# Dense products with plain fp32 operands instead of fp32r high and low parts

## The chip, the cores and the metric

The kernel runs on one core of a Trainium2 chip. The metric is the device time of one execution in microseconds. The kernel before takes 3159.32 us, the median of two runs (3153.93 and 3164.72).

## The reference

The input is 512 tokens of width 1024 in fp32. Two hybrid layers come first. Each does, with D = 1024:

```python
mod = (c @ w_ada + b_ada)                      # shifts, scales, gains from a condition vector
h = rms_norm(x) * (1 + sc_m) + sh_m
proj = h @ w_in                                # to lru, q_down, kv_down, k_rope, gate_a, gate_b
y_a = rg_lru(causal_depthwise_conv(x_lru, ...), ...)   # block gates 128x128, a scan over time
y_b = mla(q_down, kv_down, k_rope, ...)        # 8 heads, up-projections w_uq, w_ukv, softmax
x = x + g_m * ((sigmoid(gate_a) * y_a + sigmoid(gate_b) * y_b) @ w_out)
h = rms_norm(x) * (1 + sc_f) + sh_f
gate, up = split(h @ w_ffn_in)                 # 2 x 2816 columns
x = x + g_f * ((silu(gate) * up) @ w_ffn_out)
```

A second block follows: a mixer (an mLSTM of 4 heads and a pooling branch between dense products w_in_2 and w_out_2), and a mixture of 32 experts of which each token takes 4, with a SwiGLU of width 1024 in each.

## The kernel before

Activations lie transposed: 8 tiles of 128 features by 512 tokens. A dense product is made in groups: one PSUM bank takes 128 output features x 512 tokens and accumulates over 8 (down-projection: 11) blocks of 128 input features. A **chunk** of weights is 1 MB (128 x 2048 floats, two groups of 8 products), 128 x 1408 floats for the down-projection.

**High and low parts.** TensorE gets its dense operands as fp32r tiles, in two parts: the high part is a copy to fp32r, the low part is the difference. A product is three matmuls, `split3` (L187 to L191): high x high, high x low, low x high. For weights, ScalarE copies the chunk from `RAW` to `WHI` (`high`, L147) and VectorE subtracts into `WLO` (`low`, L157). `RAW` has 4 slots of 8 KB per partition, `WHI` and `WLO` 3 each. SP loads a chunk when VectorE's `low` of the chunk 4 places before is done. `feed(n + 2)` on both engines keeps the parts two chunks ahead of TensorE, and stands in each engine's program between the other work of chunk n.

For activations, ScalarE and VectorE do the same at each place: after the norms (`nh`, `HH`, `HL`, L340 to L348 and L564 to L574), for the compressed queries and keys (`cqh`, `cql`, `ckvh`, `ckvl`), for the heads' result (`yh`, `yl`), for the hidden tiles of the feed-forward (`hidh`, `hidl`, L492 and L765), and in the mixer (L1404, L1533, L1670 to L1673, L1689).

**Order.** Each engine has one program in written order, and semaphores carry the dependencies. TensorE in a layer (`layer_pe`): four lru chunks with the block gates between them (`gates`, L839; its matmul at L848 has plain fp32 operands), q, kv, four ga, four gb chunks, the value up-projection (8 products of `ckv` by token), then 8 heads, each with five `split3` products for the queries and keys of the head two later, scores, transposes and values with plain fp32 operands; four `out` chunks, column sums for the norm (`stat`, L196), 11 `fi` chunks, 8 `fo` chunks, and both again for the second half of the hidden width. The wait for `ffl` (L958) of the last hidden tile stands before each `fo` group; the wait for `yl` of the last head (L943) before `out`.

Between the weight chunks lie chunks of `w_ada`, whose columns VectorE makes (`ada`, L513) and TensorE adds up (L822). The block weights `lruw` are loaded at chunk 4 of a layer, after the previous layer's last product. POOL writes zeros into the result buffer and prepares the experts' bias terms. The mixer (`mix_program`) goes in the same way through 15 chunks: gate, 4 qk, 2 v (256 columns a product), 2 u, 2 o, 4 out.

The expert loop (`moe_pe`, products at L2274) has 50 blocks of 64 tokens. Each block has 8 chunks for gate and up and 4 for down, with 4 matmuls of plain fp32 operands in each chunk.

Of the kernel before, what the change touches and what calls it, by code (L numbers as in the profile page):

```python
# [17 lines left out]
F32R = mybir.dt.float32r  # L18
# [8 lines left out]
P = 128  # L27
D = 1024
S = 512
# [28 lines left out]
RAW_SLOTS, W_SLOTS = 4, 3  # L58
# [58 lines left out]
class Part:  # L117

    def __init__(self, sg, l, chunks, prev, used, hi):
        self.sg, self.l, self.chunks, self.prev, self.used, self.hi = sg, l, chunks, prev, used, hi  # L120
        self.pieces = [c for c in chunks if c[2]]
        self.position = {c[:2]: n for n, c in enumerate(chunks)}
        self.ada = [c[:2] for c in chunks if not c[2]]
        self.ada_after = {chunks[n - 1][:2]: self.ada.index(c[:2]) for n, c in enumerate(chunks) if not c[2]}
        self.raw_from = prev.raw_from + len(prev.chunks) if prev else 0
        self.w_from = prev.w_from + len(prev.pieces) if prev else 0
# [4 lines left out]
    def w(self, n):  # L131
        return (n + self.w_from) % W_SLOTS

    def raw_free(self, n):

        if n >= RAW_SLOTS:
            return [self.sg.event(self.used, n - RAW_SLOTS)]
        return [self.prev.sg.event(self.prev.used, len(self.prev.chunks) + n - RAW_SLOTS)] if self.prev else []

    def w_free(self, n):  # L140

        if n >= W_SLOTS:
# [12 lines left out]


def low(v, m, L, n):  # L157

    kind, i, _ = L.pieces[n]
    c, size = L.position[kind, i], FLOATS.get(kind, SLOT)  # L160
    v.wait_ge(*L.sg.event(L.hi, n))
    v.tensor_tensor(m["WLO"][:, L.w(n), 0:size], m["RAW"][:, L.raw(c), 0:size],  # L162
                    m["WHI"].bitcast(F32)[:, L.w(n), 0:size], ALU.subtract).then_inc(*L.sg.inc(L.used, c, also=[("w", n)]))


AHEAD = 2
# [40 lines left out]
def log1p(v, sg, sem, out, u, s, p):  # L207
# [20 lines left out]
LAYER_SIGNALS = """step_act step_dve raw_in0 raw_in1 raw_in2 raw_in3 vec_in lruw_in raw_used w_hi pe_step  # L228
    act_free dve_free act_out dve_out act_sq act_root act_hi dve_h dve_lo act_exp act_pt act_qk
    dve_max dve_p dve_qa dve_pt dve_y ada_out"""  # L230


def layer_loads(sp, L, start, m, W):
# [11 lines left out]
    for n, (kind, i, _) in enumerate(L.chunks):  # L245
# [61 lines left out]
FLOATS = {"fo": NF * P}  # L307
# [3 lines left out]
def layer_act(act, L, after, start, m, b):  # L311
    K, X, HH, sg = m["K"], m["X"], m["HH"], L.sg

    fed = [AHEAD if L.prev else 0]

    def feed(upto):

        while fed[0] <= min(upto, len(W_CHUNKS) - 1):
            high(act, m, L, fed[0])
            fed[0] += 1  # L320
# [7 lines left out]
    def norm(t, eps):  # L328
# [11 lines left out]
        for k in range(KD):  # L340
            if t == 0 and not L.prev and k in (0, 4):
                feed(k // 4)
            act.wait_ge(*sg.event("dve_h", ("n", t, k)))
            if k >= 2:
                act.wait_ge(*sg.event("hl", (t, k - 2)))
# [37 lines left out]
    for n, (kind, i, _) in enumerate(W_CHUNKS):  # L383
        if kind == "uq":
            break
        feed(n + 2)
# [24 lines left out]
        elif kind == "ga":  # L411
# [5 lines left out]
            if i == 1:  # L417
# [4 lines left out]
                act.wait_ge(*sg.event("cq"))  # L422
                act.activation(m["cqh"][:], m["qraw"][:], ACT.Copy)
                act.activation(m["ckvh"][:], m["kvraw"][:], ACT.Copy).then_inc(*sg.inc("act_hi", "cq"))
# [7 lines left out]
    feed(W_INDEX["ukv", 0])  # L432
# [4 lines left out]

    def rounded(h):

        act.wait_ge(*sg.event("y", h))  # L440
        act.activation(m["yh"][:, h, :], m["ya"][:, h, :], ACT.Copy).then_inc(*sg.inc("act_hi", ("y", h)))


    for h in range(-2, HEADS):
# [19 lines left out]
        if h >= 0:  # L464
# [6 lines left out]
            if h:  # L471
                rounded(h - 1)
            if h >= 6:
                feed(W_INDEX["out", h - 6])
    rounded(HEADS - 1)
    act.activation(m["warm"][:], K[:, K_ONE:K_ONE + 1], ACT.Sqrt)
    for i in range(4):
        feed(W_INDEX["out", i] + 2)
# [4 lines left out]
    for q in range(2 * NF):  # L483
        half, j = divmod(q, NF)
        feed(W_INDEX["fi", q] + 2)
# [5 lines left out]
        act.wait_ge(*sg.event("ff_hid", q))  # L491
        act.activation(m["hidh"][:, j, :], m["fh"][:, q % 2, :], ACT.Copy).then_inc(*sg.inc("act_hi", ("ff", q)))  # L492
        if j == NF - 1:
            if half:
                act.activation(m["warm"][:], K[:, K_ONE:K_ONE + 1], ACT.Sqrt)
            for jj in range(KD):
                feed(W_INDEX["fo", half * KD + jj] + 2)
                if half and jj:
                    act.wait_ge(*sg.event("dve_free", FIRST_GROUP["fo", KD + jj - 1]))
                    square(2, jj - 1)  # L500
                if half and jj >= KD - AHEAD:
                    high(act, m, after, jj - KD + AHEAD)
    act.wait_ge(*sg.event("dve_free", FIRST_GROUP["fo", 2 * KD - 1]))
    square(2, KD - 1)


def layer_dve(v, L, after, start, m, b):
    f = lambda t: t.bitcast(F32)
    K, X, HH, HL, vec, mod, sg = m["K"], m["X"], m["HH"], m["HL"], m["vec"], m["mod"], L.sg

    fed, nw = [AHEAD if L.prev else 0], [AHEAD if L.prev else 0]

    def ada():  # L513

        c = fed[0]
        r = L.ada.index(L.chunks[c][:2])
# [12 lines left out]
        fed[0] += 1  # L529

    def feed(upto):


        while nw[0] <= min(upto, len(W_CHUNKS) - 1):
            if not L.chunks[fed[0]][2]:
                ada()
                continue
            low(v, m, L, nw[0])
            nw[0] += 1
            fed[0] += 1  # L540
# [12 lines left out]
    def norm(t):  # L553
# [10 lines left out]
        for k in range(KD + 1):  # L564
            if k < KD:
                if k >= 2:
                    v.wait_ge(*sg.event("act_hi", ("h", t, k - 2)))
                v.tensor_tensor(m["nt"][:, k % 2, :], X[:, k, :], root[:], ALU.mult).then_inc(*sg.inc("dve_h", ("n", t, k)))
            if t == 0 and not L.prev and k in (1, 5):
                feed(k // 4)  # L570
            if k:
                v.wait_ge(*sg.event("act_hi", ("h", t, k - 1)))
                v.tensor_tensor(HL[:, k - 1, :], m["nh"][:, (k - 1) % 2, :], f(HH)[:, k - 1, :],  # L573
                                ALU.subtract).then_inc(*sg.inc("dve_lo", ("h", t, k - 1), also=[("hl", (t, k - 1))]))  # L574
# [68 lines left out]
    for n, (kind, i, _) in enumerate(W_CHUNKS):  # L643
# [14 lines left out]
        elif kind == "ga":  # L658
# [4 lines left out]
            if i == 1:  # L663
# [3 lines left out]
                for j in range(2):  # L667
                    v.scalar_tensor_tensor(m["qraw"][:, j, :], m["qraw"][:, j, :], vec[:, V_QG + j:V_QG + j + 1],
                                           m["rq"][:, 0, :], ALU.mult, ALU.mult)
                v.scalar_tensor_tensor(m["kvraw"][:], m["kvraw"][:], vec[:, V_KVG:V_KVG + 1], m["rq"][:, 1, :],  # L670
                                               ALU.mult, ALU.mult).then_inc(*sg.inc("dve_out", "cq", also=[("cq", None)]))
                v.wait_ge(*sg.event("cq"))
                v.wait_ge(*sg.event("act_hi", "cq"))
                v.tensor_tensor(m["cql"][:], m["qraw"][:], f(m["cqh"])[:], ALU.subtract)
                v.tensor_tensor(m["ckvl"][:], m["kvraw"][:], f(m["ckvh"])[:], ALU.subtract).then_inc(*sg.inc("dve_lo", "cq", also=[("cql", None)]))
# [9 lines left out]

    def low_y(h):

        v.wait_ge(*sg.event("act_hi", ("y", h)))
        v.tensor_tensor(m["yl"][:, h, :], m["ya"][:, h, :], f(m["yh"])[:, h, :], ALU.subtract).then_inc(*sg.inc("dve_lo", ("y", h), also=[("yl", h)]))


    for h in range(-2, HEADS):
# [25 lines left out]
        if h >= 0:  # L718
# [6 lines left out]
            if h:  # L725
                low_y(h - 1)
# [6 lines left out]
    low_y(HEADS - 1)  # L733
# [17 lines left out]
    for q in range(2 * NF):  # L751
# [5 lines left out]
        if q >= 2:  # L757
            v.wait_ge(*sg.event("act_hi", ("ff", q - 2)))
# [1700 lines left out]
```

## Time and profile before

| | |
|---|---|
| median of the runs | 3159.32 us |
| profiled execution | 3160.7 us, span 3159.0 us |
| granted clock of TensorE, mean | 0.957 |
| TensorE matmul busy | 2889.7 us, 91% |
| TensorE weight load busy | 1776.6 us, 56% |
| VectorE busy | 1243.8 us, 39% |
| ScalarE busy | 748.3 us, 24% |
| GpSimd busy | 111.2 us, 4% |
| moved by DMA | 638.66 MB, mean 202 GB/s |

All times are of one profiled execution. A busy time is the union over an engine's records. Matmul records are from start to modelled end and overlap when matmuls follow each other, so the mean of a group is longer than the distance between two starts. Layer 0 reaches its first dense product at 63.02 us, the second layer follows at about 826 us, the mixer at about 1607 us, the expert loop at about 1895 us, and the last block ends at about 3115 us.

### The profile page before, as it was taken

To read this page: it belongs to the slowest core of one execution; us is meant where nothing else is said; L and a number is where in the kernel's file an instruction comes from. 1 tells how busy PE (TensorE), PEld (TensorE's weight loads), DVE (VectorE), ACT (ScalarE), POOL (GpSimd) and SP (SyncE) were. 2 spreads that over 40 slices of the span, in tenths; PEclk is the share of its full clock that TensorE was granted. 3 is DMA by queue.
4 is the path that set the end of the run, shared out by engine and by line. 5 is a ranking of instruction groups with operands and counts; after the bars stand their busy time and mean duration, and the time that the engine had idled before them with its cause. 6 is when DMAs were issued, how large, how long until landed. Compare 5 with 4: busy or idle time off the path is not lost.

```text
span 3159.0 us, 36442 instructions
## 1 busy us (share of the span) xinstructions
PE 2889.7 (91%) x13284; PEld 1776.6 (56%) x13284; DVE 1243.8 (39%) x2119; ACT 748.3 (24%) x1068; POOL 111.2 (4%) x171
## 2 busy tenths in 40 slices
PE   6997899999999899999998979999998999998984
PEld 5775578887778667788776763333332333332221
DVE  6883656765484454334266531111111111111113
ACT  3633432122373334222232320000000000000001
POOL 0020000000000000000010000000000000000001
PEclk7999999999999999999988979999999999999997
DMA  7264136664314022242322059594699979979995
GB/s 234 80 215 132 56 109 183 193 190 124 107 56 118 14 67 67 78 116 77 90 68 85 14 200 383 202 380 150 239 408 410 395 304 408 410 301 410 410 410 197
DMA packets 392991, 638.66 MB, mean 202 GB/s; under 512 B 28400, under 2 KB 278384, under 8 KB 392896
## 3 DMA queue, kind: packets, MB, share of 16 engines
q1 hardware_dynamic: 374784, 590.76, 52.3%
q0 software_dynamic: 9376, 31.14, 2.8%
q10 hardware_dynamic: 8736, 15.47, 1.4%
q8 instruction: 63, 1.03, 0.1%
q14 instruction: 32, 0.26, 0.0%
HBM read 610.77 MB, written 26.54 MB: 202 GB/s over the span
## 4 chain that ended last, share of the span: by engine, by line
PE 72%; DVE 7%; SPq 7%; DMA 7%; ACT 5%; issue 2%; POOL 0%; ACTq 0%; DVEq 0%; another core or an unknown queue 0%
PE bank L2274 24%; PE bank L189 13%; PE bank L191 12%; PE bank L190 12%; SPq L2164 5%; DMA ring<-w_down 4%; DMA ring<-w_gate 2%; PE bank L196 1%; PE bank L2279 1%; PE bank L899 1%; PE bank L900 1%; SPq L295 1%; PE bank L2266 1%; PE bank L940 1%; DVE WLO L162 1%
## 5 line engine op out<-in xcount | busy, mean ns | idle before, releaser
L2274 PE MATMUL bank<-ring,xT 128*64 128x512 f32 x3200 | 717.7, 595 | 43.8 <-DMA ring<-w_gate 21.6
L189 PE MATMUL bank<-HH,WHI 128*128 128x512 f32 x1360 | 551.5, 406 | 34.4 <-DVE HL L573 24.8
L190 PE MATMUL bank<-HL,WHI 128*128 128x512 f32 x1360 | 534.9, 393 | 0.0
L191 PE MATMUL bank<-HH,WLO 128*128 128x512 f32 x1360 | 534.5, 393 | 0.0
L2274 PEld LDWEIGHTS bank<-ring,xT 128*64 128x64 f32 x3200 | 220.1, 137 | 490.9 <-issue 384.6
L2274 PE MATMUL bank<-ring,hT 128*64 128x512 f32 x1600 | 360.0, 595 | 27.5 <-DMA ring<-w_down 25.8
L162 DVE TENSOR_TENSOR WLO<-RAW,WHI 128x2048 fp32r<-128x2048 f32 (+1 forms) x133 | 283.1, 2128 | 134.5 <-ACT WHI L154 134.4
L189 PEld LDWEIGHTS bank<-HH,WHI 128*128 128x128 f32 x1360 | 258.5, 190 | 108.4 <-DVE HL L573 20.4
L154 ACT ACTIVATE WHI<-RAW 128x2048 fp32r<-128x2048 f32 (+1 forms) x133 | 236.6, 1779 | 238.3 <-PE bank L191 177.5
L190 PEld LDWEIGHTS bank<-HL,WHI 128*128 128x128 f32 x1360 | 259.6, 191 | 54.0 <-issue 3.7
L191 PEld LDWEIGHTS bank<-HH,WLO 128*128 128x128 f32 x1360 | 258.8, 190 | 55.2
L2237 DVE TENSOR_SCALAR gc<-bank 128x512 f32<-128x512 f32 x50 | 34.6, 692 | 616.1 <-PE bank L2274 606.9
L2274 PEld LDWEIGHTS bank<-ring,hT 128*64 128x64 f32 x1600 | 108.5, 137 | 263.2 <-issue 195.6
L2217 ACT ACTIVATE ysb<-bank 128x512 f32<-128x512 f32 x50 | 29.9, 597 | 729.0 <-PE bank L2274 729.0
L2240 DVE TENSOR_SCALAR uc<-bank 128x512 f32<-128x512 f32 x50 | 34.6, 692 | 405.4 <-PE bank L2274 405.4
L189 PE MATMUL bank<-hidh,WHI 128*128 128x512 f32 x352 | 142.5, 405 | 11.8 <-DVE hidl L765 11.8
L524 DVE SCALAR_TENSOR_TENSOR acc<-RAW,c,acc 128x256 f32<-128x256 f32 x280 | 135.8, 485 | 10.0
L190 PE MATMUL bank<-hidl,WHI 128*128 128x512 f32 x352 | 139.6, 396 | 0.0
L191 PE MATMUL bank<-hidh,WLO 128*128 128x512 f32 x352 | 139.5, 396 | 0.0
L2210 ACT ACTIVATE th<-gc 128x512 f32<-128x512 f32 x50 | 31.6, 631 | 420.9 <-DVE gc L2237 420.9
L741 DVE SCALAR_TENSOR_TENSOR X<-bank,mod,X 128x512 f32<-128x512 f32 x48 | 36.0, 750 | 180.4 <-PE bank L191 180.4
L760 DVE SCALAR_TENSOR_TENSOR fh<-fth,bank 128x512 f32<-128x512 f32 x44 | 30.3, 688 | 165.1 <-PE bank L191 116.7
(397 smaller groups left out, 2920.5 us busy)
## 6 DMA issues: line engine op xcount, KB each, us to landing
ring<-w_gate SPq DMA_DIRECT2D x128, 1024.0 KB, 11.7
ring<-w_up SPq DMA_DIRECT2D x128, 1024.0 KB, 14.3
ring<-w_down SPq DMA_DIRECT2D x128, 1024.0 KB, 15.9
RAW<-w_ffn_in SPq DMA_DIRECT2D x88, 512.0 KB, 5.2
RAW<-w_ada SPq DMA_DIRECT2D x40, 1024.0 KB, 5.3
RAW<-w_in SPq DMA_DIRECT2D x37, 1024.0 KB, 5.6
RAW<-w_ffn_out SPq DMA_DIRECT2D x32, 704.0 KB, 4.7
expert_results<-ysb ACTq DMA_DIRECT2D x102, 128.0 KB, 5.5
```

Of the source, the lines that this page charges most:

```text
L154: act.activation(m["WHI"][:, L.w(n), 0:size], m["RAW"][:, L.raw(c), 0:size], ACT.Copy).then_inc(*L.sg.inc(L.hi, n))
L162: v.tensor_tensor(m["WLO"][:, L.w(n), 0:size], m["RAW"][:, L.raw(c), 0:size], m["WHI"].bitcast(F32)[:, L.w(n), 0:size], ALU.subtract).then ...
L189: pe.matmul(out, lhi, rhi, start=start, stop=False)
L190: pe.matmul(out, lhi, rlo, start=False, stop=False)
L191: return pe.matmul(out, llo, rhi, start=False, stop=stop)
L524: ins = v.scalar_tensor_tensor(acc, raw[:, k * 256:(k + 1) * 256], m["c"][:, k:k + 1], acc, ALU.mult, ALU.add)
L741: v.scalar_tensor_tensor(X[:, k, :], b[(g + j) % 4][:], mod[:, gain + k:gain + k + 1], X[:, k, :], ALU.mult, ALU.add).then_inc(*sg.inc("dv ...
L2164: return sp.dma_start(m["ring"][:, c, :].rearrange("p (k n) -> p k n", k=2), w[:, 2 * a:2 * a + 2, :])
L2210: act.activation(m["th"][:], m["gc"][:], ACT.Tanh, scale=SWIGLU_ALPHA / 2).then_inc(*sg.inc("mo_act", also=[("th", None)]))
L2237: v.tensor_scalar(gc, b[0][:], SWIGLU_LIMIT, None, ALU.min).then_inc(*sg.inc("mo_dve", also=[("gc", None)]))
L2240: v.tensor_scalar(uc, b[1][:], SWIGLU_LIMIT, -SWIGLU_LIMIT, ALU.min, ALU.max).then_inc(*sg.inc("mo_dve", also=[("uc", None)]))
L2274: ins = pe.matmul(out[halves(h), :], xT[:, k % 4, halves(k // 4)], m["ring"][:, c, at:at + 512], start=False, stop=k == KD - 1)
```

## The change

All dense products take plain fp32 operands, one matmul in the place of the three. `WHI`, `WLO` and all high and low parts of activations go, and so do `high`, `low`, `split3` and the copies and subtractions. `RAW` gets ten slots of 8 KB, in the place of 4 + 3 + 3. TensorE waits for a chunk's DMA itself and frees its slot; only ada chunks are freed by VectorE. The norm writes `H` with one ScalarE activation in the place of two. The first group of `out` waits for each head's `y`, the first group of `fo` for each hidden tile. `lruw` is loaded at chunk 8 in the place of 4, the mixer's small tables at chunk 9 in the place of 4, and its pool and router weights before ("o", 1) in the place of ("u", 1). The expert part stays.

```diff
-RAW_SLOTS, W_SLOTS = 4, 3
+RAW_SLOTS = 10
...
+    def chunk_used(self, n):
+
+        kind, i, dense = self.chunks[n]
+        return self.sg.event("w_used", self.index[kind, i]) if dense else self.sg.event("raw_used", n)
...
+    def weights(self, pe, m, n):
+
+        kind, i, _ = self.pieces[n]
+        c = self.position[kind, i]
+        pe.wait_ge(*self.sg.event("raw", c))
+        return m["RAW"][:, self.raw(c), :]
...
-def split3(pe, out, lhi, llo, rhi, rlo, start, stop):
-
-    pe.matmul(out, lhi, rhi, start=start, stop=False)
-    pe.matmul(out, lhi, rlo, start=False, stop=False)
-    return pe.matmul(out, llo, rhi, start=False, stop=stop)
...
-        if n == 4:
+        if n == LRUW_AT:
...
-            h = dict(scale=m["mod"][:, scale + k:scale + k + 1], bias=m["mod"][:, shift + k:shift + k + 1])
-            act.activation(m["nh"][:, k % 2, :], m["nt"][:, k % 2, :], ACT.Identity, **h)
-            act.activation(HH[:, k, :], m["nt"][:, k % 2, :], ACT.Identity, **h).then_inc(*sg.inc("act_hi", ("h", t, k)))
+            act.activation(H[:, k, :], m["nt"][:, k % 2, :], ACT.Identity, scale=m["mod"][:, scale + k:scale + k + 1],
+                           bias=m["mod"][:, shift + k:shift + k + 1]).then_inc(*sg.inc("act_h", ("h", t, k)))
...
-                if norm is not None and j == 0:
-                    pe.wait_ge(*sg.event("hl", (norm, k)))
-                ins = split3(pe, out[:], hi[:, c:c + P], lo[:, c:c + P], xh[:, k, :], xl[:, k, :], k == 0, k == KD - 1)
+                if first is not None and j == 0:
+                    pe.wait_ge(*first(k))
+                ins = pe.matmul(out[:], w[:, c:c + P], x[:, k, :], start=k == 0, stop=k == KD - 1)
...
-    pe.wait_ge(*sg.event("yl", KD - 1))
     for i in range(4):
-        dense("out", i, m["yh"], m["yl"])
+        dense("out", i, m["ya"], first=None if i else lambda k: sg.event("y", k))
...
-            pe.wait_ge(*sg.event("ffl", half * NF + NF - 1))
             for k in range(NF):
-                c = k * P
-                ins = split3(pe, out[:], hi[:, c:c + P], lo[:, c:c + P], m["hidh"][:, k, :], m["hidl"][:, k, :], k == 0, k == NF - 1)
+                if j == 0:
+                    pe.wait_ge(*sg.event("ff_hid", half * NF + k))
+                ins = pe.matmul(out[:], w[:, k * P:(k + 1) * P], m["hid"][:, k, :], start=k == 0, stop=k == NF - 1)
...
-            if n == RAW_SLOTS:
+            if n == RAW_SLOTS - 1:
                 sp.wait_ge(*L.prev.sg.event("dve_free", FIRST_GROUP["fo", 2 * KD - 1]))
...
-            if (kind, i) == ("u", 1):
+            if (kind, i) == ("o", 1):
                 sp.wait_ge(*sg.event("pre", 7))
...
-        pool.wait_ge(*sg.event("hl", KD - 1))
+        pool.wait_ge(*sg.event("h", KD - 1))
```

## Rows read from the trace of the kernel before

**Rows 1.** The page: busy time by engine, and lines of the chain that ended last

```profile
PE 2889.7 (91%) x13284; PEld 1776.6 (56%) x13284; DVE 1243.8 (39%) x2119; ACT 748.3 (24%) x1068; POOL 111.2 (4%) x171
...
PE bank L2274 24%; PE bank L189 13%; PE bank L191 12%; PE bank L190 12%; SPq L2164 5%; DMA ring<-w_down 4%; DMA ring<-w_gate 2%; PE bank L196 1%; PE bank L2279 1%; PE bank L899 1%; PE bank L900 1%; SPq L295 1%; PE bank L2266 1%; PE bank L940 1%; DVE WLO L162 1%
```

**Rows 2.** Windows: busy us (x instructions) by engine, granted clock, DMA share, GB/s

```profile
63.00:1860.00 1797.00, 1688.30 (x7532) 1345.83 (x7533) 984.04 (x1583) 630.14 (x862) 36.27 (x49) 0.96 0.35 102
...
1895.00:3115.00 1220.00, 1146.52 (x5500) 384.07 (x5499) 177.95 (x350) 86.19 (x152) 57.88 (x99) 1.00 0.87 341
```

**Rows 3.** Groups by shape: the first product of each triple

```profile
L189 PE MATMUL bank<-HH,WHI 128*128 128x512 f32 x1360 | 551.5, 406 | 34.4 <-DVE HL L573 24.8 <-DVE HL L1533 4.1 <-DVE HL L1673 2.7
...
L189 PE MATMUL bank<-hidh,WHI 128*128 128x512 f32 x352 | 142.5, 405 | 11.8 <-DVE hidl L765 11.8
...
L189 PE MATMUL bank<-yh,WHI 128*128 128x512 f32 x128 | 52.2, 408 | 9.6 <-DVE yl L689 9.6
...
L189 PE MATMUL bank<-cqh,WHI 128*128 128x512 f32 x64 | 26.4, 412 | 1.9 <-ACT V L436 1.9
...
L189 PE MATMUL bank<-WHI,ckvh 128*128 128x512 f32 x16 | 7.8, 490 | 19.0 <-DVE WLO L162 14.1 <-issue 4.9
...
L189 PE MATMUL bank<-WHI,HH 128*128 128x256 f32 x64 | 18.1, 283 | 0.0
```

**Rows 4.** Timeline (start us, duration us) of the output projection, layer 0

```profile
400.36 0.39 PE L189 MATMUL bank<-yh,WHI 128*128 128x512 f32 x1
...
409.20 0.39 PE L189 MATMUL bank<-yh,WHI 128*128 128x512 f32 x1
```

**Rows 5.** Plain fp32: line L848, its weight loads in time, and L2274

```profile
L848 PE MATMUL bank<-xc,lruw x64: 590/592/593, 92.8 to 918.9; 128*128 128x512 f32 x64
...
93.20 0.19 PEld L848 LDWEIGHTS bank<-xc,lruw 128*128 128x128 f32 x1 [0.24 <-issue]
...
95.77 0.19 PEld L189 LDWEIGHTS bank<-HH,WHI 128*128 128x128 f32 x1 [0.24 <-issue]
...
L2274 PE MATMUL bank<-ring,xT 128*64 128x512 f32 x3200 | 717.7, 595 | 43.8 <-DMA ring<-w_gate 21.6
```

**Rows 6.** The page's groups: VectorE's subtractions and ScalarE's copies of weights

```profile
L162 DVE TENSOR_TENSOR WLO<-RAW,WHI 128x2048 fp32r<-128x2048 f32 (+1 forms) x133 | 283.1, 2128 | 134.5 <-ACT WHI L154 134.4
...
L154 ACT ACTIVATE WHI<-RAW 128x2048 fp32r<-128x2048 f32 (+1 forms) x133 | 236.6, 1779 | 238.3 <-PE bank L191 177.5
```

**Rows 7.** TensorE's waits: line <- releaser: us in total, times, longest us

```profile
PE bank L189 <- DVE HL L573: 24.8, 16, 8.3
...
PE bank L189 <- DVE WLO L162: 15.6, 2, 14.1
...
PE bank L189 <- DVE hidl L765: 11.8, 4, 3.1
...
PE bank L1757 <- ACT row L1429: 10.9, 1, 10.9
...
PE bank L189 <- DVE yl L689: 9.6, 2, 6.2
...
PE bank L189 <- issue: 4.9, 1, 4.9
...
PE bank L189 <- DVE HL L1533: 4.1, 5, 2.4
```

**Rows 8.** The longest wait of SP's DMA queue

```profile
SPq L295 <- DVE WLO L162: 922.2, 104, 107.5
```

**Rows 9.** Windows with low clock, same columns as Rows 2

```profile
250.00:275.00 25.00, 9.95 (x37) 7.82 (x36) 7.30 (x6) 12.46 (x15) 0.72 (x1) 0.73 0.92 271
...
385.00:437.00 52.00, 51.40 (x245) 43.39 (x245) 22.70 (x30) 12.36 (x12) 0.00 (x0) 0.95 0.49 142
...
1700.00:1800.00 100.00, 89.13 (x390) 66.09 (x391) 53.20 (x153) 35.39 (x66) 0.00 (x0) 0.90 0.10 32
```

**Rows 10.** DMA issues: count, KB each, median us to landing

```profile
RAW<-w_in SPq DMA_DIRECT2D x37, 1024.0 KB, 5.6
```

More of the change, by code:

```diff
@@ L306, with layer_act @@
 Q_ORDER = (1, 0, 2, 3)
-FLOATS = {"fo": NF * P}
 SCALE = (NOPE + ROPE) ** -0.5
[L311 to L320, printed above, removed]
+def layer_act(act, L, start, m, b):
+    K, X, H, sg = m["K"], m["X"], m["H"], L.sg
     def square(t, k):
@@ L490, in layer_act, with layer_dve @@
         act.activation(m["fth"][:, q % 2, :], b[g % 4][:], ACT.Tanh, scale=0.5).then_inc(*sg.inc("act_out", ("ff_tanh", q)))
[L491 to L511, printed above, removed]
+    act.activation(m["warm"][:], K[:, K_ONE:K_ONE + 1], ACT.Sqrt)
+    for k in range(KD):
+        act.wait_ge(*sg.event("dve_free", FIRST_GROUP["fo", KD + k]))
+        square(2, k)
+def layer_dve(v, L, start, m, b):
+    K, X, vec, mod, sg = m["K"], m["X"], m["vec"], m["mod"], L.sg
+    columns_done = [0]
     def ada():
-        c = fed[0]
-        r = L.ada.index(L.chunks[c][:2])
+        r = columns_done[0]
+        c = L.position[L.ada[r]]
         v.wait_ge(*sg.event("raw", c))
@@ L528, in ada @@
         ins.then_inc(*sg.inc("raw_used", c, also=[("ada_acc", r)]))
-        fed[0] += 1
+        columns_done[0] += 1
     def feed(upto):
[L534 to L540, printed above, removed]
+        last = L.position[W_CHUNKS[min(upto, len(W_CHUNKS) - 1)][:2]]
+        while columns_done[0] < len(L.ada) and L.position[L.ada[columns_done[0]]] < last:
+            ada()
     def modulate(bank, lo, hi, *also):
@@ L563, in norm @@
             v.wait_ge(*sg.last("step_dve"))
[L564 to L574, printed above, removed]
+        for k in range(KD):
+            if k >= 2:
+                v.wait_ge(*sg.event("act_h", ("h", t, k - 2)))
+            v.tensor_tensor(m["nt"][:, k % 2, :], X[:, k, :], root[:], ALU.mult).then_inc(*sg.inc("dve_h", ("n", t, k)))
     v.wait_ge(*sg.event("vec_in"))
@@ L773, in layer_dve @@
                     v.wait_ge(*sg.event("dve_free", FIRST_GROUP["fo", jj]))
-                if half and jj == KD - 1:
-                    for n in range(AHEAD):
-                        low(v, m, after, n)
                 residual("fo", half * KD + jj, 1, 40)
@@ L792, in bank @@
         return b[g % 4]
-    def weights(n):
-        pe.wait_ge(*sg.event("w", n))
-        return m["WHI"][:, L.w(n), :], m["WLO"][:, L.w(n), :]
     def stat(t, blocks):
@@ L823, in ada_columns, with dense @@
         ins.then_inc(*sg.inc("pe_step", also=[("ada_col", r)]))
-    def dense(kind, i, xh=HH, xl=HL, norm=None):
+    def dense(kind, i, x=H, first=None):
         n, g = W_INDEX[kind, i], FIRST_GROUP[kind, i]
-        hi, lo = weights(n)
+        w = L.weights(pe, m, n)
         for j in range(2):
@@ L853, in layer_pe @@
     for i in range(4):
-        dense("lru", i, norm=None if i else 0)
+        dense("lru", i, first=None if i else lambda k: sg.event("act_h", ("h", 0, k)))
         if i:
@@ L879, in layer_pe @@
         tok, c = slice((j // 2) * P, (j // 2 + 1) * P), 1024 + (j % 2) * 512
-        ins = split3(pe, out[:], m["ckvh"][:, tok], m["ckvl"][:, tok], ukv_hi[:, c:c + 512], ukv_lo[:, c:c + 512], True, True)
+        ins = pe.matmul(out[:], m["ckv"][:, tok], ukv[:, c:c + 512], start=True, stop=True)
         ins.then_inc(*sg.inc("pe_step", also=[("acc", g + j)]))
@@ L905, in layer_pe @@
             a = h + 2
-            hi, lo = weights(W_INDEX["uq", a // 4])
+            uq = L.weights(pe, m, W_INDEX["uq", a // 4])
             if a:
@@ L910, in layer_pe @@
                 c = k * 1024 + (a % 4) * 256
-                ins = split3(pe, b[3][:], hi[:, c:c + P], lo[:, c:c + P], m["cqh"][:, k, :], m["cql"][:, k, :], k == 0, k == 1)
+                ins = pe.matmul(b[3][:], uq[:, c:c + P], m["cq"][:, k, :], start=k == 0, stop=k == 1)
             ins.then_inc(*sg.inc("pe_step", also=[("qn_acc", a)]))
@@ L916, in layer_pe @@
                 c = k * 1024 + (a % 4) * 256 + P
-                ins = split3(pe, b[4][:], hi[:, c:c + P], lo[:, c:c + P], m["cqh"][:, k, :], m["cql"][:, k, :], k == 0, k == 1)
+                ins = pe.matmul(b[4][:], uq[:, c:c + P], m["cq"][:, k, :], start=k == 0, stop=k == 1)
             ins.then_inc(*sg.inc("pe_step", also=[("qr_acc", a)]))
@@ L951, in layer_pe @@
         for j in range(NF):
-            dense("fi", half * NF + j, norm=None if half or j else 1)
+            dense("fi", half * NF + j, first=None if half or j else lambda k: sg.event("act_h", ("h", 1, k)))
         for j in range(KD):
@@ L1481, in mix_program @@
             ins.then_inc(*sg.inc("mix_out_act", also=[("hn_act", h)]))
-        for h in range(MH):
-            act.wait_ge(*sg.event("ym", h))
-            act.activation(HH[:, h, :], m["hm"][:, h, :], ACT.Copy).then_inc(*sg.inc("mix_out_act", also=[("ymh", h)]))
         def square(k):
@@ L1830, in out_part @@
         def out_part(k, half):
-            hi, lo = weights("out", k // 2)
+            w = weights("out", k // 2)
             if half == 0:
@@ L1841, in out_part @@
                 d = 4 + j if half == 0 else j
-                pe.wait_ge(*sg.event("yml" if half else "ypl", j))
+                if half:
+                    pe.wait_ge(*sg.event("ym", j))
+                    y = m["hm"][:, j, :]
+                else:
+                    pe.wait_ge(*sg.event("emptied", ("pool", j)))
+                    y = m["yp"][:, j, :]
                 c = d * 256 + (k % 2) * P
-                ins = split3(pe, b[k % 4][:], hi[:, c:c + P], lo[:, c:c + P], HH[:, d, :], HL[:, d, :], d == 4, d == 3)
+                ins = pe.matmul(b[k % 4][:], w[:, c:c + P], y, start=d == 4, stop=d == 3)
             if half:
```

221 lines of the change are left out of this document (50 added, 171 removed).

## The prediction

> **What bounds the kernel now.** I read the page's busy times first. TensorE is busy 2889.7 of 3159.0 us, VectorE 39% and ScalarE 24%, and the chain of work that ended last is mostly TensorE's, with the three lines of `split3` at 12 to 13% each [rows 1]. So the question is what one dense product costs TensorE in either form, and only then what the other engines give back.
>
> The windows view divides the time. From 63 to 1860 us, the two layers and the mixer, TensorE is busy 1688.3 of 1797 us; the expert loop from 1895 to 3115 us already uses plain fp32 operands, the change doesn't touch it, and its DMA share is 0.87 [rows 2]. I leave everything after 1860 us as it is. The whole effect must come out of the first 1797 us.
>
> **The products: what goes.** Every dense product is three matmuls on fp32r tiles. The groups by shape give how many: 1360 + 352 + 128 + 64 + 16 + 16 = 1936 triples with 512 columns (of the two groups of 16 one is shown), and 64 with 256 columns [rows 3]. The durations in those rows (about 400 ns) are from start to end and overlap, so they are not the price. The price is the distance between starts. In the timeline of an output projection, 13 triples lie between the starts at 400.36 and 409.20 us: 8.84 / 13 = 0.680 us a triple, 0.227 us a matmul [rows 4].
>
> **The products: what comes.** One plain fp32 matmul of 128x128 weights on 128x512. The trace has this very operation in the block gates at L848, and here one must count. The code runs 2 layers x 8 blocks x 2 gates = 32 such matmuls, and the trace shows 64 records [rows 5]: one plain fp32 matmul is two records. Their weight loads start at 93.20 and, six records later, at 95.77 us: 2.57 / 6 = 0.428 us a record [rows 5], so 0.857 us a matmul. Reading 590 ns as the price of one, beside three times 400, would turn the sign round.
>
> So each triple goes from 0.680 to 0.857 us, +0.177 us, and 1936 x 0.177 = **+342 us**. For the 64 with 256 columns no row is used; half of the difference is my estimate, 64 x 0.09 = +6 us (between 0 and 11, the full difference). At half clock both forms take twice as long, so the ratio stands. Together +348 us, all on TensorE, which has no room to hide it.
>
> The Trainium skill, "FP8 and Floating Point Precision", section TensorE Precision Notes, says that true fp32 takes four passes through the array. The rows agree that it takes more than three fp32r products, but 0.857 / 4 = 0.214 us a pass is less than the 0.227 us between fp32r matmuls [rows 4, 5]. Four passes at the fp32r distance are a rival below.
>
> **The rounding and subtracting: what goes.** Per weight chunk one ScalarE copy (WHI, 236.6 us in all) and one VectorE subtraction (WLO, 283.1 us) [rows 6], and the same for activations. They lie beside TensorE, so their busy time is worth nothing by itself. What they are worth is TensorE's idle time that they ended [rows 7]:
> - WLO 15.6 us, of which 14.1 is one stall at the up-projection of keys and values: I take all of it. Loads now hold ten slots and are freed by TensorE, where SP's queue waited 922.2 us for WLO subtractions [rows 8], so the slow w_uq pieces arrive early.
> - HL of the layers 24.8 us over 16 stalls. One activation copy and the subtraction leave the chain, and the first product no longer waits for a weight subtraction (2.3 us). The root, the multiplication and one ScalarE activation remain before the first product; I leave 10 and take 14.8.
> - hidl 11.8 us: the down-projection now asks for each hidden tile separately, so ten products (8.6 us) cover the last one. All taken.
> - yl 9.6 us: the output projection can start on the first seven heads, 6 us of work, while the last is finished. All taken.
> - ACT row at L1757 10.9 us: the gate's row chain on VectorE had subtractions queued between its steps, and TensorE's work over it gets longer. I take 9.
> - "issue" before L189 4.9 us: it stands before the same up-projection in the second layer. All taken.
> - HL at L1533 4.1 us: I take 2.6.
>
> Sum 68 us. The last tenths of each are guesses; the bound is all the idle time of the stretch, 1797 - 1688.3 = 109 us, plus the 8.3 us before the first product [rows 2, 7].
>
> **The clock.** Granted clock from 63 to 1860 us is 0.96 of full [rows 2]: 0.04 x 1797 = 72 us lost at half clock. Part of it follows the stalls just removed: 25 x 0.27 = 7 us in 250 to 275, 52 x 0.05 = 3 around the output projection and as much in the second layer, half of 100 x 0.10 in 1700 to 1800 [rows 9]. I take 18 us back. The low clock behind the norms' column sums stays, since those stay.
>
> **Moved waits.** TensorE now waits for the DMA of a chunk itself. A chunk of 16 products takes 16 x 0.857 = 13.7 us of TensorE and 5.6 us to land [rows 10]; with ten slots that is free, and if a load were late, one such landing per late chunk would be the cost. The block weights (lruw) and the mixer's small tables go later in SP's queue, behind 8 and 9 chunks. Lruw still waits for the end of the previous layer's last product and is first needed two chunks (27 us) later; behind that wait stand chunks needed 8 x 13.7 us later. The pool weights move two places in the queue, still behind the eighth convolution. I cost all three at nothing. The ada columns on VectorE keep their place and lose neighbours. POOL waits for h, which comes earlier.
>
> **Sum.** 3159 + 348 - 68 - 18 = **3421 us** on the span. The profiled execution took 3160.7 us beside its span of 3159.0, and the median of the runs is 3159.3, so the same figure holds for the median. That is 8% slower. (About 2% is what a measurement of this kernel tells from no change.)
>
> **Rivals.**
> 1. The waits don't go, they change name: the ends of the norms, the head softmax and late chunks stop TensorE instead. Against it: the copies really leave the chains. With 20 us back instead of 86: 3487 us. Chance 0.12.
> 2. Everything comes back: no idle time and no low clock in the stretch, 3159 + 348 - 117 - 72 = 3318 us; half way, 3370. Against it: the attention heads' waits for softmax and copies, and the norms, aren't touched. Chance 0.06.
> 3. The other side, faster: the plain product in a stream of accumulations costs one record, 0.428 us, because the second record is peculiar to L848. Then 1936 x (0.680 - 0.428) = 488 us go, and 3159 - 488 - 86 = 2585 us. It decides as soon as one product costs under 0.680 us. Against it: the same shape and types, back to back, and the gate and up products of the expert loop have 3200 records where the code has 50 blocks x 32 = 1600 products [rows 5]. Chance 0.03.
> 4. Four passes at 0.227 us, because weights change every product as they do for the triples: 0.907 us, +0.227 x 1936 = 439, plus 8 - 86: 3520 us. Against it: L848 changes weights each time as well. The page of the Trainium skill named above gives the four passes, and no distance between them. Chance 0.04.
>
> **Numbers.** Forecast 3421, chance 0.74 (0.01 is left for none of these). The range 3375 to 3490 reaches from the half-way point of rival 2 to rival 1. Slower by over 2% (above 3222): 0.96, from every case but the third; within 2%: 0.01; faster: 0.03.
>
> **What would show it.** Dense products as two records 0.43 us apart, 2 x 1936 of them; TensorE busy near 3200 us; VectorE down by at least 283 us and ScalarE by at least 237 with no gain from that; stalls under HL, WLO, hidl and yl gone, with short ones on the activation of the norm; the expert loop still 1220 us long. The prediction is wrong if the distance between starts is not 0.857 us, if TensorE waits on weight DMAs for more than 20 us before the expert loop, or if that loop changes length.

## The result: 7.5% slower, because a plain product costs more than three fp32r products

The changed kernel takes 3395.93 us (median of 2 runs, 3393.34 to 3398.51), against 3159.32 us before: ratio 1.0749, 95% interval 1.0662 to 1.0835. Measured again beside experiments, it takes 3391.68 us (4 runs) against 3159.06 us (7 runs): 1.0738, interval 1.0720 to 1.0756. The forecast was 3421 us, range 3375 to 3490.

The page after begins with TensorE busy 310 us more, VectorE 351 us less and ScalarE 294 us less than in [rows 1]:

```profile
span 3391.5 us, 31696 instructions
...
PE 3199.6 (94%) x11284; PEld 1405.0 (41%) x11284; DVE 892.9 (26%) x1874; ACT 454.3 (13%) x823; POOL 111.0 (3%) x171
```

Of the chain of work that ended last, 84% is TensorE's, and one line, L732, the plain product, stands where the three of `split3` stood. VectorE's share of it is 2%:

```profile
PE 84%; DMA 6%; SPq 5%; DVE 2%; issue 1%; ACT 1%; POOL 0%; ACTq 0%; DVEq 0%; POOLq 0%; another core or an unknown queue 0%
PE bank L732 33%; PE bank L2098 23%; PE bank L857 9%; SPq L1988 5%; DMA ring<-w_down 3%; PE bank L1569 2%; DMA ring<-w_gate 2%; PE bank L1595 2%; PE bank L1668 2%; PE bank L172 1%; PE bank L2103 1%; PE bank L796 1%; PE bank L837 1%; PE bank L797 1%; PE bank L808 1%
```

**The stretches.** The columns of the windows are those of [rows 2]: length, busy us (x instructions) of TensorE, weight loads, VectorE, ScalarE and POOL, granted clock, DMA share, GB/s. The first row runs from the first dense product to 1 or 2 us behind the last of the mixer's router products. The same stretch of before is the first row of [rows 2], less its last 2 us (1795 us, busy 1686.3).

```profile
60.60:2091.00 2030.40, 1996.65 (x5519) 973.54 (x5520) 633.07 (x1319) 337.67 (x617) 35.46 (x49) 0.98 0.30 88
80.00:455.00 375.00, 368.34 (x1082) 181.35 (x1080) 173.22 (x364) 107.69 (x202) 23.07 (x32) 1.00 0.37 112
485.00:940.00 455.00, 453.37 (x1190) 212.42 (x1188) 138.08 (x274) 18.97 (x32) 0.00 (x0) 1.00 0.47 137
```

So the stretch grew from 1795 to 2030.4 us, by 235 us. TensorE's idle time in it went from 108.7 to 33.8 us. The expert loop starts 233.0 us later (2128.3 against 1895.3 us) and the span grew by 232.5 us: nothing changed behind the stretch. (The first dense product starts 2.4 us earlier, 60.60 against 63.02 us. Experiments on the kernel before start it anywhere from 59.9 to 63.2 us, with the same stall in front of it, so I make nothing of that.)

**The products.** Groups by shape, with counts that are now records: 2304 + 704 + 256 and eight smaller groups, 3872 in all, two for each of the 1936 products of 512 columns. The 64 products of 256 columns are 128 records.

```profile
L732 PE MATMUL bank<-H,RAW 128*128 128x512 f32 x2304 | 1007.2, 597 | 11.1 <-ACT H L312 11.1
...
L857 PE MATMUL bank<-hid,RAW 128*128 128x512 f32 x704 | 307.1, 594 | 0.0
L732 PE MATMUL bank<-ya,RAW 128*128 128x512 f32 x256 | 111.4, 594 | 0.0
...
L1564 PE MATMUL bank<-RAW,H 128*128 128x256 f32 x128 | 27.8, 379 | 0.0
```

The price is again the distance between starts, here of the weight loads in a down-projection: 2.57 us for six records, 0.428 us each, 0.857 us a product, just what L848 showed in [rows 5].

```profile
640.36 0.19 PEld L857 LDWEIGHTS bank<-hid,RAW 128*128 128x128 f32 x1 [0.24 <-issue]
...
642.93 0.19 PEld L857 LDWEIGHTS bank<-hid,RAW 128*128 128x128 f32 x1 [0.24 <-issue]
```

**The waits** that are left in the stretch, the answers to [rows 7]:

```profile
PE bank L732 <- ACT H L312: 11.1, 4, 5.8
...
PE bank L830 <- ACT PT L424: 8.7, 16, 1.5
PE bank L1576 <- ACT row L1301: 8.6, 1, 8.6
...
PE bank L1569 <- DVE H L1369: 0.9, 1, 0.9
```

WLO, hidl, yl and the "issue" before the up-projection are gone, and no dense product waits for a weight DMA. HL (24.8 us) became the norm's activation (11.1 us). The mixer's row chain stands nearly as before (8.6 us for 10.9).

### The profile page after: what moved, and what is told of

Read it like the earlier page. It is cut to its first block, busy times and chain, and to the rows that moved or that the text cites. A ratio compares the mean times of both kernels' runs of the same rounds, so it can differ in the third digit from the quotient of the medians.

```text
span 3391.5 us, 31696 instructions
## 1 busy us (share of the span) xinstructions
PE 3199.6 (94%) x11284; PEld 1405.0 (41%) x11284; DVE 892.9 (26%) x1874; ACT 454.3 (13%) x823; POOL 111.0 (3%) x171
## 4 chain that ended last, share of the span: by engine, by line
PE 84%; DMA 6%; SPq 5%; DVE 2%; issue 1%; ACT 1%; POOL 0%; ACTq 0%; DVEq 0%; POOLq 0%; another core or an unknown queue 0%
PE bank L732 33%; PE bank L2098 23%; PE bank L857 9%; SPq L1988 5%; DMA ring<-w_down 3%; PE bank L1569 2%; DMA ring<-w_gate 2%; PE bank L1595 2%; PE bank L1668 2%; PE bank L172 1%; PE bank L2103 1%; PE bank L796 1%; PE bank L837 1%; PE bank L797 1%; PE bank L808 1%
## 5 line engine op out<-in xcount | busy, mean ns | idle before, releaser
L732 PE MATMUL bank<-H,RAW 128*128 128x512 f32 x2304 | 1007.2, 597 | 11.1 <-ACT H L312 11.1
L732 PEld LDWEIGHTS bank<-H,RAW 128*128 128x128 f32 x2304 | 439.1, 192 | 554.7 <-issue 550.6
L2098 PE MATMUL bank<-ring,hT 128*64 128x512 f32 x1600 | 361.7, 597 | 27.8 <-DMA ring<-w_down 26.2
L857 PE MATMUL bank<-hid,RAW 128*128 128x512 f32 x704 | 307.1, 594 | 0.0
L857 PEld LDWEIGHTS bank<-hid,RAW 128*128 128x128 f32 x704 | 132.3, 190 | 159.3 <-issue 158.8
L437 ACT ACTIVATE fth<-bank 128x512 f32<-128x512 f32 x44 | 26.3, 597 | 719.8 <-PE bank L732 719.8
L732 PE MATMUL bank<-ya,RAW 128*128 128x512 f32 x256 | 111.4, 594 | 0.0
L732 PEld LDWEIGHTS bank<-ya,RAW 128*128 128x128 f32 x256 | 48.1, 190 | 57.9 <-issue 57.6
L1569 PE MATMUL bank<-H,RAW 128*128 128x512 f32 x160 | 71.1, 607 | 0.9 <-DVE H L1369 0.9
L296 ACT ACTIVATE sq<-X 128x512 f32<-128x512 f32 x32 | 20.1, 630 | 278.0 <-DVE X L652 247.9
L1595 PE MATMUL bank<-H,RAW 128*128 128x512 f32 x128 | 56.8, 598 | 0.0
```

The costliest lines, as they stand in the source:

```text
L732: ins = pe.matmul(out[:], w[:, c:c + P], x[:, k, :], start=k == 0, stop=k == KD - 1)
L857: ins = pe.matmul(out[:], w[:, k * P:(k + 1) * P], m["hid"][:, k, :], start=k == 0, stop=k == NF - 1)
L1569: ins = pe.matmul(o[:], w[:, c:c + P], H[:, k, :], start=k == 0, stop=k == KD - 1)
L1595: ins = pe.matmul(o[:], w[:, c:c + P], H[:, k, :], start=k == 0, stop=k == KD - 1)
L2098: ins = pe.matmul(out[halves(h), :], xT[:, k % 4, halves(k // 4)], m["ring"][:, c, at:at + 512], start=False, stop=k == KD - 1)
```

## The experiments

All ratios are to runs of the kernel before on the same chip, which took 3157 to 3159 us. Experiment 5 and the second half of 9 ran on one chip, where the changed kernel took 3391.68 us; the others ran on a second one, where only the kernel before was measured beside them.

**1. The plain products alone, in the kernel before**

```diff
-    pe.matmul(out, lhi, rhi, start=start, stop=False)
-    pe.matmul(out, lhi, rlo, start=False, stop=False)
-    return pe.matmul(out, llo, rhi, start=False, stop=stop)
+    return pe.matmul(out, lhi.bitcast(F32), rhi.bitcast(F32), start=start, stop=stop)
```

> The kernel before, with its slots, copies, subtractions and waits as they are; only the three fp32r matmuls of a product become one plain fp32 matmul on the high parts (the low parts are made and waited for, but take no part in a product). Theory: the price of a product is the whole loss, 1936 x 0.177 + 64 x 0.074 = 347 us on a span of 3159, and what TensorE's own slowness covers comes back: the stall at the keys' and values' up-projection (14 + 5), the mixer's row chain (9) and the low clock behind them (about 10). About 3465 us, with 1936 products of two records each, 0.857 us from start to start. Rival: the stalls were given back by the removed copies alone; then they stay, and it takes 3500 us. If the plain product were cheaper in a stream than at the block gates, it would be under 3420 us.

Measured: 3476.95 us, ratio 1.1007 (1.0985 to 1.1028). The group of 1360 triples became 2720 records, and the stretch to the last router product, which took 1795 us, takes 2111 us:

```profile
L189 PE MATMUL bank<-HH,WHI 128*128 128x512 f32 x2720 | 1198.1, 599 | 28.0 <-DVE HL L571 21.8 <-DVE HL L1531 3.0 <-DVE HL L1671 2.2
```

```profile
60.00:2171.00 2111.00, 2026.30 (x5518) 981.59 (x5519) 980.07 (x1561) 628.59 (x858) 36.52 (x49) 0.97 0.29 86
```

Its waits (TensorE's line <- releaser: us, times, longest) show that the stalls on the weight parts shrank, from 15.6 + 4.9 to 9.4 us, and HL and the row chain by 2 to 3 us each. Those on hidl and yl stayed, or grew a little, against [rows 7]:

```profile
PE bank L189 <- DVE HL L571: 21.8, 13, 8.3
...
PE bank L189 <- DVE hidl L763: 11.8, 4, 3.1
PE bank L189 <- DVE yl L687: 11.2, 2, 7.8
...
PE bank L189 <- issue: 9.4, 2, 4.9
...
PE bank L1755 <- ACT row L1427: 8.6, 1, 8.6
```

It follows that the swap of the products costs 318 us with everything else in place. By the theory 347 us is their price. 24 us of it come back as idle time (108.7 to 84.7 us) because a slower TensorE covers more: besides those above, two waits of 3.7 and 3.6 us (on VectorE's ada columns and on ScalarE's squares for the norm of the compressed queries) are gone. Some 5 to 7 us are left for the clock. The measured time lies between theory and first rival: I had 28 us of stalls going away at the up-projections and in the row chain, and 13 went. The remaining 81 us down to the changed kernel are what the rest of the change is worth.

**2. Four slots in the changed kernel**

```diff
-RAW_SLOTS = 10
+RAW_SLOTS = 4
...
-LRUW_AT = 8
+LRUW_AT = 4
```

> The changed kernel with four weight slots in the place of ten (block weights again at chunk 4, the mixer's tables at chunk 3). Theory: the ten slots are worth only the stall at the up-projections: 10 to 30 us more than the changed kernel, all of it before the heads of layer 0 and the low clock after it. Rival: 13.7 us of TensorE per chunk hide every load with four slots too, and the time stays within 5 us.

Measured: 3410.64 us, ratio 1.0802 (1.0784 to 1.0820), 15 to 19 us over the changed kernel (3395.93 and 3391.68). Two stalls come back, one of them at the value up-projection (L777) and one on a gate chunk before it:

```profile
PE bank L732 <- DMA RAW<-w_in: 6.7, 1, 6.7
PE bank L777 <- issue: 6.1, 1, 6.1
```

These two are 12.8 us, and behind each of them the clock is low for some 5 us:

```profile
247.00:260.00 13.00, 7.35 (x11) 3.28 (x12) 0.28 (x1) 0.00 (x0) 0.72 (x1) 0.61 1.02 349
288.00:297.00 9.00, 6.94 (x10) 3.05 (x11) 0.00 (x0) 2.20 (x4) 0.00 (x0) 0.62 0.51 153
```

The rival, that four slots hide every load, falls for layer 0 alone. Layer 1 makes the same loads with four slots and has neither stall. What layer 0 has besides is POOL's writes of zeros (issued from 220 to 259 us here), with a DMA share of 1.02 in the first of these rows. So the ten slots may be worth only what these writes delay; no run has four slots with the zeros moved.

**3. Late waits in the changed kernel**

```diff
+    pe.wait_ge(*sg.event("y", KD - 1))
     for i in range(4):
-        dense("out", i, m["ya"], first=None if i else lambda k: sg.event("y", k))
+        dense("out", i, m["ya"])
...
+            pe.wait_ge(*sg.event("ff_hid", half * NF + NF - 1))
             for k in range(NF):
-                if j == 0:
-                    pe.wait_ge(*sg.event("ff_hid", half * NF + k))
```

> The changed kernel, but the output projection waits for the last head's y before its first product, and each down-projection group waits for the last hidden tile. Theory: four stalls of about 2.5 us before the down-projections and two of 2 to 4 us before the output projections come back, about 16 us, and behind some of them the clock falls for a few us: 15 to 30 us more than the changed kernel. Rival: TensorE's queue hides such short waits, 0 to 5 us.

Measured: 3403.81 us, ratio 1.0781 (1.0763 to 1.0799), 8 to 12 us more. The stalls are 11 us, less than the 16 expected, since without the copies the last hidden tile comes 1.5 us after TensorE asks, not 2.5:

```profile
PE bank L857 <- DVE hid L670: 6.0, 4, 1.7
...
PE bank L732 <- DVE ya L644: 5.0, 2, 3.5
```

A miss against the expected 15 to 30 us: the size of the stalls, and hardly any low clock behind them. The longest, of 3.5 us, ends at 392.19 us and has low clock behind it; the four at the down-projections, of 1.3 to 1.7 us, have none. The first two end at 621.58 and 857.67 us; the granted clock is 1.00 from 1491 to 1515 and from 1720 to 1745 us, around the others.

```profile
392.00:396.00 4.00, 3.81 (x6) 1.71 (x7) 3.75 (x9) 0.00 (x0) 0.00 (x0) 0.58 0.00 0
600.00:940.00 340.00, 337.34 (x891) 158.11 (x889) 96.59 (x191) 13.68 (x22) 0.00 (x0) 1.00 0.46 133
```

**4. The long chain of the norms in the changed kernel**

```diff
-            act.activation(H[:, k, :], m["nt"][:, k % 2, :], ACT.Identity, scale=m["mod"][:, scale + k:scale + k + 1],
-                           bias=m["mod"][:, shift + k:shift + k + 1]).then_inc(*sg.inc("act_h", ("h", t, k)))
+            if k >= 2:
+                act.wait_ge(*sg.event("hl", (t, k - 2)))
+            h = dict(scale=m["mod"][:, scale + k:scale + k + 1], bias=m["mod"][:, shift + k:shift + k + 1])
+            act.activation(m["nh"][:, k % 2, :], m["nt"][:, k % 2, :], ACT.Identity, **h)
+            act.activation(H[:, k, :], m["nt"][:, k % 2, :], ACT.Identity, **h).then_inc(*sg.inc("act_h", ("h", t, k)))
...
+                v.wait_ge(*sg.event("act_h", ("h", t, k - 1)))
+                v.tensor_tensor(m["HL"][:, k - 1, :], m["nh"][:, (k - 1) % 2, :], m["H"][:, k - 1, :],
+                                ALU.subtract).then_inc(*sg.inc("dve_lo", ("h", t, k - 1), also=[("hl", (t, k - 1))]))
...
-        dense("lru", i, first=None if i else lambda k: sg.event("act_h", ("h", 0, k)))
+        dense("lru", i, first=None if i else lambda k: sg.event("hl", (0, k)))
```

> The changed kernel with the long chain of the layers' norms put back: two ScalarE activations and a VectorE subtraction per tile, and TensorE's first group waits for the subtraction (whose result nothing reads). Theory: each of the four norms costs 1.5 to 5.5 us, least where TensorE runs at half clock and is slower than the chain: 6 to 22 us in all. Rival: the column sums and the root before it set the time of a norm, 0 to 3 us.

Measured: 3405.22 us, ratio 1.0782 (1.0764 to 1.0800), 9 to 14 us more. The wait is 19.2 us over 12 stalls where the changed kernel has 11.1 us over 4:

```profile
PE bank L740 <- DVE HL L505: 19.2, 12, 7.2
```

**5. The three together**

The edits of 2, 3 and 4 in one kernel, and the changed kernel once more beside it. Of the edits only the first is shown again:

```diff
-RAW_SLOTS = 10
+RAW_SLOTS = 4
...
-LRUW_AT = 8
+LRUW_AT = 4
```

> The changed kernel with four slots, the late waits and the long norm chain together. Theory: the three costs measured alone (15 + 8 + 9 us) lie at different places and add: 3425 to 3432 us; what is left to the kernel with plain products alone (3477) are the longer chains of yl, hidl and the weight parts. Rival: stalls near each other share one low clock, or one hides the other: under 3420.

> The changed kernel itself, beside the next two on the same chip: 3396 us within 5.

Measured: 3437.44 us, ratio 1.0885 (1.0866 to 1.0903), and the changed kernel beside it 3391.68 us. Together they cost 45.8 us. Alone, against the same 3391.68 us, they cost 19.0 + 12.1 + 13.5 = 44.6 us: they add. By the ratios, which compare each with the kernel before on its own chip, they are 20, 14 and 14 us alone and 46 together; each carries about 6 us of uncertainty. The expected 3425 to 3432 us was too low only because I had counted from the earlier 3395.93 us. From 3437 to the 3477 us of experiment 1, 40 us stay without an experiment of their own, so what makes them is not shown. What experiment 1 has besides are the copies and subtractions at yl, hidl and the mixer and the weight parts made two chunks ahead.

**6. Only the high product in the kernel before**

```diff
-    pe.matmul(out, lhi, rhi, start=start, stop=False)
-    pe.matmul(out, lhi, rlo, start=False, stop=False)
-    return pe.matmul(out, llo, rhi, start=False, stop=stop)
+    return pe.matmul(out, lhi, rhi, start=start, stop=stop)
```

> The kernel before with only the first of the three fp32r matmuls of a product; the low parts are made and waited for, but take no part. Theory: TensorE alone would go down by 1936 x 0.454 + 64 x 0.24 = 894 us to 2265; with TensorE at 3.6 us a chunk VectorE (2.3 us of subtraction, 3.9 us of an ada chunk, the tiles) and ScalarE become the bound, and it takes 2400 to 2600 us. That would show that the copies were free only beside slow products. Rival: they stay free, under 2330 us.

Measured: 2690.78 us, ratio 0.8524 (0.8505 to 0.8543): 425 us more than TensorE's own saving would give (1936 x 0.454 + 64 x 0.24 = 894 us off 3159, or 2265 us), and more than the 2600 us expected. VectorE is now the busier engine in the stretch, and TensorE waits for its weight parts, its hidden tiles and its ada columns:

```profile
60.00:1387.00 1327.00, 913.03 (x3522) 664.80 (x3523) 976.91 (x1566) 618.63 (x859) 37.81 (x49) 0.81 0.47 137
```

```profile
PE bank L189 <- DVE WLO L162: 70.9, 16, 32.2
PE bank L189 <- DVE fh L758: 61.7, 33, 2.3
PE bank L820 <- DVE acc L522: 49.2, 23, 13.3
```

The copies and subtractions were free only beside slow products. Of the 425 us, 305 are idle time (414 us in the stretch, against 108.7) and 120 are busy time (913 us, where 1686.3 less the 894 leaves 792): the granted clock is 0.81, which I had not put in the sum.

**7. Early waits in the kernel before**

```diff
-    pe.wait_ge(*sg.event("yl", KD - 1))
     for i in range(4):
-        dense("out", i, m["yh"], m["yl"])
+        dense("out", i, m["yh"], m["yl"], first=None if i else lambda k: sg.event("yl", k))
...
-            pe.wait_ge(*sg.event("ffl", half * NF + NF - 1))
             for k in range(NF):
+                if j == 0:
+                    pe.wait_ge(*sg.event("ffl", half * NF + k))
```

> The kernel before with three fp32r matmuls a product, but the first output group waits for each head's low part and the first down-projection group for each hidden tile's. Theory: of 9.6 + 11.8 us of stalls about 18 go, and the low clock behind them gives 5 to 12 more: 3125 to 3140 us. Rival: the wait only moves to the last tile, 0 to 5 us gained.

Measured: 3126.87 us, ratio 0.9903 (0.9887 to 0.9920): 30.5 us less (25 to 36 by the interval), for 21.4 us of stalls of which 1.3 us are left. The idle time of the stretch is 87.8 us, 20.9 less than before:

```profile
60.00:1822.00 1762.00, 1674.21 (x7521) 1335.32 (x7522) 981.28 (x1565) 627.52 (x859) 36.17 (x49) 0.96 0.35 104
```

So stalls of this kind have a second price, below.

**8. The zeros later in the kernel before**

```diff
-                eng.wait_ge(*layers[0].sg.event("kp"))
+                eng.wait_ge(*layers[0].sg.event("s", 0))
```

> The kernel before, but POOL writes its zeros (32 x 256 KB) from the first scores of layer 0 on, not beside the loads of w_uq and w_ukv. Theory: the 14 us stall there is contention with these writes; it goes, with half of the 14 us of low clock behind it: 3137 to 3145 us. Rival: w_uq is slow by its small pieces and by the slots that come free late; the stall stays at 10 us or more.

Measured: 3149.89 us, ratio 0.9977 (0.9966 to 0.9988), 7.5 us less (4 to 11 by the interval), short of the 12 to 20 us expected. POOL's writes beside the loads made most of the 14 us stall: the slowest load of `w_uq` took 23.5 us to land, and with the zeros moved none takes over 4.3 us (min, median, max, first of the kernel before, then of this one):

```profile
DMA to landing us min/median/max: 3.2/4.1/23.5
...
DMA to landing us min/median/max: 3.2/3.8/4.3
```

But 4.5 us of the stall stay under another name, as 4.9 us do in the second layer ("issue", two times):

```profile
PE bank L189 <- issue: 9.4, 2, 4.9
...
PE bank L189 <- DVE WLO L162: 1.5, 1, 1.5
```

I read them as the weight parts of the value up-projection, which need the slot of the last gate chunk; the second half of experiment 9 tests it. So neither theory nor rival had it whole.

**9. Both, and both with the keys' and values' chunk first**

First the edits of 7 and 8 in one kernel:

> The kernel before with the early waits and the later zeros together. Theory: the two gains add, 3100 to 3120 us, and this beats both kernels. Rival: they don't add, because the clock that one gives back the other had already.

Measured: 3116.28 us, ratio 0.9876 (0.9859 to 0.9892). The gains of 7 and 8 add (30.5 + 7.5 = 38.0, measured 41.1).

Then, on top of these, the order of the chunks turned round:

```diff
-    out += [("uq", 0), ("uq", 1), ("ukv", 0)]
+    out += [("ukv", 0), ("uq", 0), ("uq", 1)]
...
-    feed(W_INDEX["ukv", 0])
+    feed(W_INDEX["uq", 1])
```

> The kernel before with the early waits, the later zeros, and the chunk for keys and values ahead of the two for queries, so that its parts are made while the last gate products run. Theory: the two stalls before the value up-projection (4.9 us in each layer) go, with some low clock: 3100 to 3110 us. Rival: the query chunk behind it is then late by as much, 3114 to 3119.

Measured: 3105.61 us, ratio 0.9832 (0.9816 to 0.9848). Both "issue" stalls are gone from its waits, as that reading asks. It beats both kernels, by 53 us the kernel before: the stretch takes 1742 us, with 73 us of idle time:

```profile
60.00:1802.00 1742.00, 1669.19 (x7524) 1332.10 (x7525) 983.02 (x1569) 626.86 (x860) 36.16 (x49) 0.97 0.36 105
```

## Why the prediction was right

The mechanism was the one that was forecast: the products cost more than the whole loss, and ended stalls and low clock gave part of it back. Two things were off, the size of the clock term and the cause of the row chain's wait.

**The products** (+348 us predicted). The count of records at L848 was right, and so was the distance: 0.857 us measured. For 256 columns, where I had halved the difference, the 128 records take 27.8 us against 64 x 3 x 0.12 = 23 us for the triples: +5 us, not 6. So the term is 347 us, and experiment 1 shows it with nothing else changed. Rival 3 (one record) and rival 4 (four passes at 0.227 us) fall by the 0.428 us between records. Of the four passes that the Trainium skill gives in "FP8 and Floating Point Precision", section TensorE Precision Notes, the trace shows the total, 0.857 us; it doesn't show the passes apart.

**Idle time** (-68 us predicted). By the wait list WLO 15.6, hidl 11.8, yl 9.6 and "issue" 4.9 went whole, HL gave 13.7 for 14.8 predicted and L1533 3.2 for 2.6. In all the stretch has 75 us less idle time, since small waits that I had left out went as well. The largest, in the kernel before:

```profile
PE bank L822 <- DVE acc L524: 3.7, 1, 3.7
PE bank L863 <- ACT ti L410: 3.6, 1, 3.6
PE bank L940 <- DVE ya L732: 3.3, 2, 1.6
```

That 68 came so near to 75 is partly luck: the row chain, below, was 7 us too high, and these and smaller waits made up for it. Which part of the change gives the idle time is measured for some of it, each with the clock behind it: slots 15 to 20 us, per-tile waits 8 to 14, the norm's chain 9 to 14. Experiment 1 shows that 24 us need no more than the slower products.

**The row chain** (9 us predicted, 2.3 measured): a mistake of cause. I had the subtractions between its steps. The chain on VectorE starts only after ScalarE's exp, which stands behind the evictions of the first value chunk:

```profile
1904.20 0.39 ACT L1295 ACTIVATE v<-bank 128x256 f32<-128x256 f32 x1 [3.07 <-PE bank L1564]
1904.48 0.61 ACT L1298 ACTIVATE row<-row 4x512 f32<-4x512 f32 x1
...
1905.12 0.42 DVE L185 TENSOR_SCALAR row<-row 4x512 f32<-4x512 f32 x1 [9.87 <-ACT row L1298]
```

TensorE then has just the four groups of the second value chunk over it, 32 products, 32 x 0.074 = 2.4 us more than before. That is the whole gain, and experiment 1, with every subtraction in place, has the same 8.6 us left. TensorE's rows beside it, the value products and the waiting transposes:

```profile
1890.18 27.79 PE L1564 MATMUL bank<-RAW,H 128*128 128x256 f32 x128
1926.53 1.01 PE L1576 MATMUL bank<-K,row 4*128 4x4 f32 x8 [8.56 <-ACT row L1301]
```

**The clock** (-18 us predicted, about -37 measured): the term that was mis-sized. 347 - 75 - 235 = 37 us is what is left of the balance, a remainder and no direct measurement. The granted clock agrees as far as its two digits go: 0.96 of 1795 us is 72 us lost, 0.98 of 2030 us is 41, so 31 us less. From 80 to 455 us the changed kernel has 1.00 (above), where before had

```profile
80.00:430.00 350.00, 316.15 (x1367) 239.46 (x1366) 229.50 (x404) 148.17 (x231) 23.11 (x32) 0.96 0.39 120
```

I had given back only what followed the longest stalls. Short ones cost as well. At the first down-projection of before, a stall of 2.78 us ends at 577.56 us, and the matmuls behind it are 0.43 us apart (the lower level, 1.2 GHz) until 580.7 us, then 0.23 (2.4 GHz):

```profile
577.56 0.76 PE L189 MATMUL bank<-hidh,WHI 128*128 128x512 f32 x1 [2.78 <-DVE hidl L765]
...
579.40 0.63 PE L190 MATMUL bank<-hidl,WHI 128*128 128x512 f32 x1
579.83 0.63 PE L191 MATMUL bank<-hidh,WLO 128*128 128x512 f32 x1
...
583.31 0.39 PE L189 MATMUL bank<-hidh,WHI 128*128 128x512 f32 x1
583.54 0.39 PE L190 MATMUL bank<-hidl,WHI 128*128 128x512 f32 x1
```

That stall has 2.78 us of idle time, and the matmuls behind it, at half clock until 580.7 us, cost about 1.6 us more. Experiment 7 says the same in time: 30.5 us for 20.9 us of idle time. The low clock after the norms' column sums stayed, as predicted. In the other direction, the stalls of 1.3 to 1.7 us at the down-projections of experiment 3 leave the clock alone.

**The rest.** The moved loads cost nothing, and no dense product waited for a DMA with ten slots. The copies' busy time has no price of its own that shows: ScalarE spends what it gained in waiting for products. Before its tanh of the feed-forward it now waits 719.8 us in all, where it waited 79.5 us.

```profile
L437 ACT ACTIVATE fth<-bank 128x512 f32<-128x512 f32 x44 | 26.3, 597 | 719.8 <-PE bank L732 719.8
```

Rival 1 (the waits change name) falls, since the kernel is 91 us faster than its 3487. Rival 2 (everything comes back) holds in part: of its 189 us 112 came back where 68 + 18 were forecast, and these 26 us are why the measured times are 25 to 29 us under the forecast.

## What to carry to other kernels

Price a matmul form by the distance between starts of the same form elsewhere in the trace, and count its records against the calls in the code: here one plain fp32 product is two records, 0.857 us, and three fp32r products are 0.680 us. Work on engines beside the bound is worth only the stalls that it ends, but add to each stall of 2 to 4 us about half as much again for TensorE's clock (30.5 us for 20.9 here). When a change that loses carries a good part (here waits per tile), take that part alone: it gave 1% to the kernel that was there (experiment 7). The copies and subtractions were free only while three products stood beside them: with one, they kept the kernel 425 us above TensorE's own saving (experiment 6).

## What the runs showed of the hardware

- At full clock fp32r matmuls of 512 columns start 0.227 us apart and those of 256 columns 0.120 us; plain fp32 records start 0.428 us apart at 512 columns and 27.8 / 128 = 0.217 us at 256.
- A stall of 2.8 us in otherwise dense fp32r work was followed by some 3 us at the lower clock level, and one of 3.5 us in plain fp32 work had low clock behind it; stalls of 1.3 to 1.7 us at the down-projections of experiment 3 had none.
- With POOL's 8 MB of zeros beside it, a load of `w_uq` took up to 23.5 us to land, 4.3 us without them, and the kernel lost 7.5 us by it. Moved to the heads, where the DMA share was 0.08 and less, they end no wait of TensorE's. That they cost nothing there isn't shown: 9.6 us of stall went, and the kernel gained 7.5.
